# Three reordered calls on VectorE between the residual LayerNorm and the first attention head pair

## The reference, cut to what matters

```
x = layer_norm(ALPHA * x + (1 + gate) * mlp(x * (1 + scale) + shift))     # layer 0
p = x @ kv_w + kv_b
k, v = p[..., :1024], p[..., 1024:2048]            # 16 heads of 64
logf = log_sigmoid(p[..., 2048:])                  # 16 columns, one per head
c = cumsum(logf)                                   # over the positions
h = x * (1 + scale) + shift;  q, z = split(h @ fa_w_in + fa_b_in)
o = softmax(q k^T / 8 + c_q - c_k, causal) v
y = layer_norm(ALPHA * x + (1 + gate) * ((o * silu(z)) @ fa_w_out + b))
```

## Time and profile before

| | us |
|---|---|
| median of three runs (lowest, highest) | 1778.37 (1777.73, 1781.38) |
| the profiled execution, its own time | 1777.73 |
| its span in the trace | 1776.3 |
| PE busy | 1656.2 (93%) |
| DVE busy | 1010.4 (57%) |
| ACT busy | 623.9 (35%) |
| POOL busy | 419.0 (24%) |

### The profile page before, as it was taken

One profiled execution on the slowest core, in us unless ns is written; L12 is line 12 of the kernel. 1 busy time (PEld: TensorE's weight loads), 2 busy tenths in 40 slices (PEclk: granted clock), 3 DMA queues, 4 the chain that ended last, 5 costly groups with the idle time before them and its releaser, 6 DMA issues.

```text
span 1776.3 us, 27940 instructions
## 1 busy us (share of the span) xinstructions
PE 1656.2 (93%) x10096; PEld 1434.5 (81%) x10096; DVE 1010.4 (57%) x1568; ACT 623.9 (35%) x980; POOL 419.0 (24%) x432
## 2 busy tenths in 40 slices
PE   6999989999999988999889999999999999867976
PEld 4899989999999988999767777777777877655742
DVE  3433254334333347225567676767768686899875
ACT  2212122111121226225443645545464636451121
POOL 0000011011011010002132434425162524444221
PEclk8999999999999998999999999999999999988986
DMA  8111112212222212224323112221212121338667
GB/s 359 36 48 35 47 60 96 83 63 91 83 78 75 84 59 87 96 100 149 95 86 116 60 60 60 71 71 59 82 36 83 56 74 36 99 120 303 223 248 298
DMA packets 50191, 180.45 MB, mean 102 GB/s; under 512 B 6522, under 2 KB 8186, under 8 KB 48850
## 3 DMA queue, kind: packets, MB, share of 16 engines
q1 hardware_dynamic: 31650, 116.11, 19.3%
q0 software_dynamic: 18480, 63.53, 9.9%
HBM read 154.07 MB, written 17.15 MB: 96 GB/s over the span
## 4 chain that ended last, share of the span: by engine, by line
PE 75%; DVE 11%; issue 5%; ACT 3%; DMA 3%; POOL 2%; POOLq 1%; SPq 0%; DVEq 0%; ACTq 0%
PE bank L1684 19%; PE bank L1686 18%; PE bank L1685 18%; PE bank L2046 2%; PE bank L2000 2%; PE bank L2048 2%; PE bank L2047 2%; PE bank L1819 2%; PE bank L2028 1%; PE bank L2027 1%; DVE bank L1384 1%; DMA fsw<-units 1%; POOL p_lo L533 1%; PE bank L1799 1%; PE bank L1903 1%
## 5 line engine op out<-in xcount | busy, mean ns | idle before, releaser
L1684 PE MATMUL bank<-h_hi,w_lo 128*128 128x344 f32 x1152 | 374.5, 325 | 9.9 <-DVE h_lo L1076 8.7
L1685 PE MATMUL bank<-h_lo,w_hi 128*128 128x344 f32 x1152 | 369.0, 320 | 0.0
L1686 PE MATMUL bank<-h_hi,w_hi 128*128 128x344 f32 x1152 | 368.7, 320 | 0.0
L533 POOL TENSOR_TENSOR p_lo<-parg,p_hi 128x512 fp32r<-128x512 f32 (+1 forms) x192 | 214.0, 1132 | 173.0 <-ACT p_hi L919 172.5
L1684 PEld LDWEIGHTS bank<-h_hi,w_lo 128*128 128x128 f32 x1152 | 217.6, 189 | 14.8 <-issue 12.3
L1684 PE MATMUL bank<-x_hi,w_lo 128*128 128x512 f32 x528 | 220.8, 418 | 6.6 <-POOL x_lo L485 6.5
L1685 PEld LDWEIGHTS bank<-h_lo,w_hi 128*128 128x128 f32 x1152 | 217.8, 189 | 0.2 <-issue 0.2
L1686 PEld LDWEIGHTS bank<-h_hi,w_hi 128*128 128x128 f32 x1152 | 217.6, 189 | 0.0
L1686 PE MATMUL bank<-x_hi,w_hi 128*128 128x512 f32 x528 | 208.8, 395 | 0.0
L1685 PE MATMUL bank<-x_lo,w_hi 128*128 128x512 f32 x528 | 208.7, 395 | 0.0
L1684 PE MATMUL bank<-y_hi,w_lo 128*128 128x320 f32 (+2 forms) x512 | 180.6, 353 | 29.6 <-DVE w_lo L1034 19.0
(11 more groups left out here) (301 smaller groups left out, 2644.5 us busy)
## 6 DMA issues: line engine op xcount, KB each, us to landing
raw<-units SPq DMA_DIRECT2D x121, 512.0 KB, 3.4
ada_ring<-w_ada SPq DMA_DIRECT2D x32, 512.0 KB, 3.3
pages<-cache_k POOLq DMA_DIRECT2D x32, 512.0 KB, 5.0
pages<-cache_v POOLq DMA_DIRECT2D x32, 512.0 KB, 7.8
ada_first<-w_ada SPq DMA_DIRECT2D x8, 1024.0 KB, 14.9
ckb<-scr_c POOLq DMA_DIRECT2D x16, 512.0 KB, 4.5
KX<-KA SPq DMA_DIRECT2D x32, 256.0 KB, 4.3
xT<-x_t SPq DMA_DIRECT2D x2, 2064.0 KB, 23.3
```

Of the source, the lines that this page charges most:

```text
L533: g.tensor_tensor(p_lo[:, r, off:HALF], parg[:, r, off:HALF], p_hi[:, r, off:HALF].bitcast(F32), ALU.subtract).then_inc(S("p_ready"), 1)
L1684: mm(out, lhs_lo, rhs_hi, start=first, stop=False)
L1685: mm(out, lhs_hi, rhs_lo, start=False, stop=False)
L1686: return mm(out, lhs_hi, rhs_hi, start=False, stop=last)
```

## The change

Three calls in DVE's stream move; nothing is added or removed, and no other engine's order changes. `split_lo(0, 0)`, the subtraction for the keys' unit of head pair 0, goes from between the statistics of tiles 5 and 6 to behind those of tile 7. `take_samples(0, 1)` and `evac_s(0, 1)`, the decode rows of the queries' unit, go from ahead of the logf combination to behind the scan and its scaling.

```
@@ -1288,7 +1288,6 @@
             dve.wait_ge(S("r_ready"), 2 * KB)
             layer_norm_stats(5, 0)
-            split_lo(0, 0)
             layer_norm_stats(6, 0)
             x1_back(5)
@@ -1452,6 +1451,7 @@
             layer_norm_stats(7, 0)
+            split_lo(0, 0)
             x1_back(6)
@@ -1471,8 +1471,6 @@
             evac_s(0, 0)
-            take_samples(0, 1)
-            evac_s(0, 1)
             dve.wait_ge(S("f_act"), 2)
             v.scalar_tensor_tensor(fp[:, :], fp[:, :], 0.0, fe[:, :], ALU.min, ALU.subtract).then_inc(S("f_step"), 1)
...
             v.tensor_scalar(fc[:, :], fc[:, :], -1.0 / SCALE, None, ALU.mult).then_inc(S("f_step"), 1)
 
+            take_samples(0, 1)
+            evac_s(0, 1)
             split_lo(0, 2)
```

## The result

The median of five runs of the changed kernel is 1791.25 us (1788.35 to 1793.59). Five runs of the kernel before on the same chip had 1778.37 (1773.57 to 1781.38). The ratio is 1.0066, with a 95% interval of 1.0047 to 1.0085: slower by 8.4 to 15.1 us. The forecast was 1791.0, range 1784 to 1795. All 20 executions of the changed kernel on record, the profiled one among them, lie between 1783.40 and 1795.75 us, with a median of 1790.2. The profiled execution after took 1788.97 us, with a span of 1787.5.

The account below looks back on a forecast made before the run. PE was taken as the bound (75% of the chain of waits). First move 4.5, second move 4.8 and two slow-clock stretches 4.0 sum to 13.3 us on the profiled 1777.73: forecast 1791 us, range 1784 to 1795.

Parts of the forecast that it names:

- PE's unit late behind the transposes of tile 7: PE's keys' unit waits for the moved subtraction and starts at 890.81 instead of 885.16, 5.65 us late.
- second gap, ended by POOL `x_lo`: PE's old 6.52 us gap before the second-half products stays, at about 5.4 us.
- gap at the fold, ended by DVE `samp`: New PE gap of about 5.8 us before folding the queries' decode rows, which wait for the moved copy.
- two more slow stretches: Both new PE gaps bring the 1.2 GHz clock level, 2.0 us each, 4.0 us together, between 0 and 4.6.
- sum at the seam: From the start of tile 7's transposes on PE to the first peak product: 13.3 us added.
- rest of the kernel: Behind that stretch nothing gives the time back; the whole rest of the kernel shifts.
- First move: Keys' subtraction behind tile 7's statistics: gains 0, delays PE's unit, the old gap swallows only 1.1; costs 4.5 us.
- The blocked instruction: DVE's 128x1 `lnm` of tile 7 is held by POOL's `x_lo(5)`; without it `lnm` ends 1.7 us earlier.
- Second move: Queries' decode rows behind the scan: gains 0, PE's fold 6.0 us late; costs 4.8 us, between 4.3 and 5.4.
- The clock does not fall: Rival: the two new gaps bring no slow clock; sum 9.3 us, 1787.0, or 7.0 us, 1784.7; chance 0.22.
- One of the two waits is swallowed: Rival: only one of the moves' PE waits costs time, giving 1784.5 or 1784.2 us; chance 0.12.
- The end gives it back: Rival: PE's 14.2 us of value-cache page waits near the end absorb the cost; 1777.7 us, no change; chance 0.03.

Follow-up runs that it names:

- after_warm: Changed kernel plus matmuls nobody reads in PE's three gaps, DVE's order unchanged; 1782.66 us, ratio 1.0039 to the kernel before.
- before_warm: Kernel before plus 25 matmuls nobody reads in PE's only large gap; 1776.18 us, ratio 0.9996.
- after_again: The changed kernel run and profiled once more, unchanged; 1791.28 us, ratio 1.0077 to the kernel before.
- m1_mid: Kernel before with the keys' subtraction moved only behind the statistics of tile 6; 1777.86 us, ratio 1.0008.
- m1_pe_early: Kernel before with only the keys' subtraction moved as in the change, and PE's transposes of tiles 6 and 7 put ahead of its wait; 1775.94 us, ratio 0.9997.
- m1_only: Kernel before with only the keys' subtraction moved behind the statistics of tile 7; 1783.05 us, ratio 1.0038.
- lo3_dve: Kernel before with `x_lo` of tiles 5, 6, 7 on DVE, PE's transposes reordered and 9 unread matmuls in the gap; 1775.04 us, ratio 0.9983.
- m2_only: Kernel before with only the queries' decode rows (`take_samples`, `evac_s`) moved behind the scan; 1786.81 us, ratio 1.0062.
- before_again: The kernel before run and profiled once more, unchanged; 1778.12 us, ratio 0.9996.
- m2_evac_only: Kernel before with only `evac_s(0, 1)` moved behind the scan, `take_samples(0, 1)` left in place; 1778.86 us, ratio 1.0013.
- before_warm_dve: Kernel before with the last tile's `x_lo` on DVE instead of POOL and 17 unread matmuls in PE's gap; 1775.15 us, ratio 0.9987.

## Why the prediction was right

| step | forecast, us | measured, us |
|---|---|---|
| PE's unit late behind the transposes of tile 7 | 5.65 | 5.5 (6.37 after their start; before 0.85, 885.16 less 884.31) |
| gap in front of it | 5.4 | 5.28 |
| first move without clock | 4.5 | 4.54 (after_warm) |
| second gap, ended by POOL `x_lo` | 5.4 | 5.41 |
| gap at the fold, ended by DVE `samp` | 5.8 | 5.73 |
| both moves without clock | 9.3 | 9.2 (after_warm less before_warm) |
| two more slow stretches | 4.0 | 3.5 (5.7 for all three, less the old one's 2.2 before) |
| sum at the seam | 13.3 | 12.7; 13.6 in after_again |
| rest of the kernel | 0 | -7.3 in the first trace; within the scatter in the second (841.8 against 842.1 and 840.05) |

**What bounds the kernel.** PE at the seam was the right place to look, and PE's fixed order was the argument that decided. m1_mid and m1_pe_early show it from two sides: the same DVE move with PE not waiting, and the same DVE move with PE's queue turned, both leave the second half where it was, 14.93 and 14.99 us after the transposes.

**First move.** The chain of the prediction (late unit, late transposes, POOL's store and `x_lo` pushed back, 1.1 of 5.65 us swallowed) stands row by row in the profile after, and m1_only shows it alone. One small term came without a row: 0.14 us from DVE's end to PE's start. Here it was 0.06 and 0.05.

**The blocked instruction.** `lnm` of tile 7 took 1.85 us after, ended with POOL's `x_lo(5)` again, and in lo3_dve, where POOL has no such product, 0.16. What the earlier trace rows could only suggest from two ends within 0.05 us is now shown by taking the partner away: it then ended 3.5 us after the start of the transposes (890.47 less 886.99) instead of 5.2, the 1.7 us that the prediction has. That a VectorE instruction with two SBUF inputs and a GpSimd instruction that reads SBUF exclude each other for the whole instruction is what the Trainium skill says ("SBUF — State Buffer", section "Who interferes with whom"), and these traces agree.

**Second move.** The gap was 5.73 us for 5.8. The 0.55 us wait for the low part of the queries went away as forecast: L2000 has no wait in after and in m2_only. The reason given holds too: before, POOL's scaling of the next unit ran from 929.87 to 931.78 into the two subtractions that end in the queries' low part (`QA`, from 930.93), and they took 3.19 us; in m2_only it was done at 938.61, ahead of them (939.00), and they took 2.47. Both warm kernels together leave 9.24 less 4.54 = 4.7 for this move, where 4.8 was taken.

**The clock.** Three slow stretches came, as forecast, but not of one size, and this is the term that was sized least well. Behind the first gap the twelve matmuls took 4.84 us (896.43 to 901.27) against 2.90 in after_warm (894.15 to 897.05): 1.9. Behind the third, from the fold to the transposes of `fc`, 7.77 against 5.29: 2.5. Behind the second, six matmuls took 2.72 (911.36 to 914.08) where six at the full clock take 1.4: 1.3, and the stretch was 3.4 us long instead of 6.8. The parts that lay behind the gaps, 4.3, 3.0 and 5.5 us, are at half speed worth 2.2, 1.5 and 2.7, near the 1.9, 1.3 and 2.5 measured. So the old stretch, which the prediction left at 2.3, gave 0.9 us back (its work to the decode rows took 8.99 us, before 9.90). The sum is 12.7 in one profile and 13.6 in the other, where the three were 0.4, 0.25 and 0.15 us dearer. The mean of 2.0 for each was right for a sum of three, and by luck as much as by the rows: their lengths were not to be seen ahead.

**The rivals.** *The clock does not fall* (0.22) fell on the PEclk rows, and after_warm shows what it would have been: 56.92, 5.7 us less. *One of the two waits is swallowed* (0.12) fell with m1_only and m2_only, each of which costs its own. *The end gives it back* (0.03) had the first profile on its side, 7.3 us, and fell with after_again and before_again, and with the runs: the middles of the two ratios are 11.7 and 13.7 us, as much as the seams show. Had I taken the span alone, 11.2 us more, I would have said that the sum was 2 us too high; it was right at the seam, and the span had two errors of chance in it, +5.75 ahead and -7.3 behind. That the forecast of 1791.0 met the median to 0.25 us is luck: the kernel's own executions scatter by 12 us, and the clock term alone was off by 0.5.

What stays open: m2_only's ratio (7.8 to 14.2 us) has its middle 3.3 us above what its seam shows, and m2_evac_only's 2.1 below. Both seams lie at the edge of their intervals (7.75 just outside, 4.4 just inside). And all four kernels with a shorter seam gained less in time than at the seam: by the middles of their ratios 0.7, 0.5, 2.3 and 3.0 us (before_warm, m1_pe_early, before_warm_dve, lo3_dve), where the seams have 2.2, 2.2, 3.9 and 5.8. More runs would be needed to say whether that is scatter, or whether the rest of the kernel takes some of a gain back.

## What to carry to other kernels

When an instruction is moved on an engine that has time to spare, look on the engine that waits for it, at what stands behind that wait in its own order: the same lateness cost 5.4 us with twelve matmuls and a transpose queued behind it, and nothing with the transposes ahead. Price each new gap of PE twice, once for its length and once for the part of the slow stretch that lies behind it (1.3 to 3.0 us here). To judge a change of a few us in a kernel whose runs scatter by 10, measure the distance between two fixed events around it, and take a second profile before you believe that something is given back elsewhere.

## What the runs showed of the hardware

- **Gaps of one length, slow stretches of several.** At gaps of 5.3 to 6.5 us the granted clock was 0.50 for 3.4 us (after, second gap), 6.8 us (before) or 10.2 us (m1_mid, at the fold of m2_only). It fell while PE was still idle, 0.4 us (after, second gap) to 4.4 us (m1_mid) before PE resumed. A gap of 2.7 us ahead of the seam, which every kernel has, brought 3.4 us of slow clock after, where it did not before (874.71); it did in ten of the thirteen traces. PE's timeline after:

```profile
879.89 1.62 PE L1843 MATMUL bank<-ident,rT 128*128 128x128 f32 x8 [2.68 <-DVE rT L1287]
...
882.60 0.63 PE L1684 MATMUL bank<-x_hi,w_lo 128*128 128x512 f32 x1
...
884.70 0.40 PE L1685 MATMUL bank<-x_lo,w_hi 128*128 128x512 f32 x1
```

The busy time of a matmul of 512 columns is 0.63 us at the slow level and 0.40 at the full one. So two executions of one kernel can differ by some us here without any difference in order.
- **Idle PE time can be filled for the clock's sake.** With matmuls whose result is not used in the gap the clock stayed at 1.00 behind it: the seam lost 2.2 us with one gap and 5.7 us with three. They cost nothing where they end before the awaited event; the waits left were 0.27 to 0.90 us.
- **A small instruction can be blocked for as long as a large one of another engine runs**: 1.85 and 1.89 us for a 128x1 operation on DVE beside POOL's 128x1024 product, 0.16 without it. Where such an instruction is on the last stretch before a wait of PE, moving the product away brought its end forward by 1.7 us (lo3_dve).
